# A hybrid decoder layer on one core: each head's values product placed behind the next round's sums of decays

## What is computed

```python
# differential attention, 8 heads, per head h and block of 128 queries
logits = q @ k.T ; logits = where(dist >= 0, logits + bias, -inf)
p = softmax(logits)                         # two maps per head
attn = p[:, :, 0] - lam * p[:, :, 1]
out = attn @ v[:, :kend]                    # the "values product"
...
# state-space branch, 32 heads in 4 groups, chunks of 128 tokens
acs = cumsum(a)                             # a = dt*A: the decays
decay_in = exp(where(causal, acs_l - acs_s, -inf))
y_diag = einsum(cb, decay_in, xs)
```

## Time and profile before

| | us |
|---|---|
| median of 3 runs | 989.04 |
| lowest, highest | 988.66, 990.14 |
| the profiled execution, whole time | 989.82 |
| the profiled execution, span from first to last instruction | 987.7 |
| span of the eight rounds, from the first sums of decays | 154.2 to 288.6 |

### The profile page before, as it was taken

How to read it: one execution, slowest core, us unless ns; L and a number is a source line. 1 busy time by engine, 2 the same in 40 slices (tenths; PEclk the granted TensorE clock), 3 DMA queues, 4 the chain that set the end, 5 groups by cost and what they waited for, 6 DMA issues and landing times.

```text
span 987.7 us, 15502 instructions
## 1 busy us (share of the span) xinstructions
PE 972.6 (98%) x6366; PEld 700.5 (71%) x6367; DVE 516.1 (52%) x1051; ACT 392.1 (40%) x707; POOL 53.4 (5%) x54
## 2 busy tenths in 40 slices
PE   9999999999999999999999999999999999999995
PEld 8999999999999999999984444444444444444342
DVE  6988555767679976765675433223222232222124
ACT  6776435656577743555341122112211221122113
POOL 0000102324200000000000000000000000000000
PEclk9999999999999999999999999999999999999998
DMA  8584534333354554656969999999999999999993
GB/s 315 187 307 174 197 139 140 124 125 126 129 176 166 186 198 172 241 211 255 405 253 362 415 420 419 420 420 420 419 420 420 419 420 420 420 420 420 421 419 122
DMA packets 42982, 292.43 MB, mean 296 GB/s; under 512 B 4760, under 2 KB 6944, under 8 KB 8352
## 3 DMA queue, kind: packets, MB, share of 16 engines
q1 hardware_dynamic: 42128, 286.19, 73.3%
q0 software_dynamic: 784, 5.24, 1.4%
HBM read 290.36 MB, written 2.63 MB: 297 GB/s over the span
## 4 chain that ended last, share of the span: by engine, by line
PE 89%; SPq 5%; DMA 3%; DVE 2%; issue 0%; ACT 0%; DVEq 0%; ACTq 0%
PE stream L1631 33%; PE stream L1988 19%; PE stream L2012 10%; PE stream L1656 9%; PE work L1977 5%; SPq L532 5%; DMA place_w<-in_wstream 3%; PE stream L1998 1%; PE stream L1929 1%; PE work L1755 1%; PE stream L1937 1%; PE stream L1931 1%; PE stream L1935 1%; PE work L1731 1%; PE work L1862 1%; PE work L1844 1%
## 5 line engine op out<-in xcount | busy, mean ns | idle before, releaser
L1032 DVE TENSOR_TENSOR w_lo<-raw,w_hi 128x1024 fp32r<-128x1024 f32 x142 | 172.4, 1233 | 54.0 <-ACT w_hi L699 53.7
L1988 PE MATMUL stream<-ring,xg 128*64 128x512 f32 x640 | 197.3, 593 | 1.7 <-DMA ring<-in_wstream 1.0
L699 ACT ACTIVATE w_hi<-raw 128x1024 fp32r<-128x1024 f32 x142 | 147.3, 1052 | 58.4 <-DMA raw<-in_wdense 41.5
L1631 PE MATMUL stream<-xT_hi,w_hi 128*128 128x256 f32 x560 | 159.4, 285 | 0.0
L1631 PE MATMUL stream<-xT_lo,w_hi 128*128 128x256 f32 x560 | 157.9, 282 | 0.0
L1631 PE MATMUL stream<-xT_hi,w_lo 128*128 128x256 f32 x560 | 157.8, 282 | 0.0
L1988 PEld LDWEIGHTS stream<-ring,xg 128*64 128x64 f32 x640 | 62.6, 137 | 92.2 <-issue 92.2
L1631 PEld LDWEIGHTS stream<-xT_hi,w_hi 128*128 128x128 f32 x560 | 106.1, 190 | 3.7 <-issue 3.1
L1631 PEld LDWEIGHTS stream<-xT_hi,w_lo 128*128 128x128 f32 x560 | 105.9, 189 | 0.0
L1631 PEld LDWEIGHTS stream<-xT_lo,w_hi 128*128 128x128 f32 x560 | 105.6, 189 | 0.0
L1502 DVE TENSOR_TENSOR hh<-h,stream 128x256 f32<-128x256 f32 x32 | 13.5, 421 | 173.3 <-ACT h L961 173.3
(11 more groups left out here) (389 smaller groups left out, 2019.4 us busy)
## 6 DMA issues: line engine op xcount, KB each, us to landing
ring<-in_wstream SPq DMA_DIRECT2D x120, 1024.0 KB, 19.4
raw<-in_wdense SPq DMA_DIRECT2D x72, 1024.0 KB, 4.8
place_e<-in_wstream SPq DMA_DIRECT2D x24, 1024.0 KB, 19.1
place_m<-in_wstream SPq DMA_DIRECT2D x12, 1024.0 KB, 17.6
place_c<-in_wstream SPq DMA_DIRECT2D x12, 1024.0 KB, 19.5
place_w<-in_wstream SPq DMA_DIRECT2D x12, 1024.0 KB, 19.1
place_x<-in_wstream SPq DMA_DIRECT2D x12, 1024.0 KB, 21.2
ln<-in_lnp POOLq DMA_DIRECT2D x3, 1024.0 KB, 7.0
```

The lines of the kernel that those rows point to most:

```text
L699: nc.scalar.activation(w_hi[:, q % ROUNDED, :], raw[:, q % 6, :], ACT.Copy).then_inc(w_rounded, 1)
L1032: tt(w_lo[:, q % 6, :], raw[:, q % 6, :], w_hi[:, q % ROUNDED, :].bitcast(F32), ALU.subtract).then_inc(w_rest, 1)
L1631: last = mm(S[n % 4][:, 0:SEQ], w[:, b, :], a[:, kb, :], start=(kb + j == 0), stop=(kb == chunks * KB - 1 and j == len(parts) - 1))
L1988: last = mm(S[2][e * SLOTS:(e + 1) * SLOTS, :], feature_block(buf, kb)[:, col + e * SLOTS:col + (e + 1) * SLOTS], tiles[e][kb // 4][:, kb ...
```

## The change

The three values products become a function `values(i)`. It is called for head i-1 in round i, behind the sums of decays and in front of the wait for `av_cp`, and once for head 7 behind the loop. Nothing is added or taken away; the wait for `attnT_cp` that the logits had moves into the function.

```diff
+            def values(i):
+                pe.wait_ge(attnT_cp, i + 1)
+                head = slice(i * P, (i + 1) * P)
+                mm(W[1][:, 0:P], attnT[:, 0:P], v[:, 0, head], start=True, stop=True)
+                mm(W[1][:, P:SEQ], attnT[:, P:SEQ], v[:, 0, head], start=True, stop=False)
+                mm(W[1][:, P:SEQ], attnT[:, SEQ:384], v[:, 1, head], start=False, stop=True).then_inc(av_mm, 1)
...
                 if i >= 1:
-                    pe.wait_ge(attnT_cp, i)
+                    values(i - 1)
                     pe.wait_ge(av_cp, i)
...
                 if i == 0:
                     pe.wait_ge(act_took, taken_count(out_index("v", 7)))
-                pe.wait_ge(attnT_cp, i + 1)
-                head = slice(i * P, (i + 1) * P)
-                mm(W[1][:, 0:P], attnT[:, 0:P], v[:, 0, head], start=True, stop=True)
-                mm(W[1][:, P:SEQ], attnT[:, P:SEQ], v[:, 0, head], start=True, stop=False)
-                mm(W[1][:, P:SEQ], attnT[:, SEQ:384], v[:, 1, head], start=False, stop=True).then_inc(av_mm, 1)
+            values(7)
```

## The result

| | before | after |
|---|---|---|
| median of 6 runs each, us | 988.85 | 993.00 |
| lowest, highest, us | 988.54, 990.14 | 991.79, 993.86 |
| ratio after/before, 95% interval | | 1.0039 [1.0026, 1.0052] |
| the profiled execution, whole time, us | 989.82 | 992.59 |
| its span, us | 987.7 | 990.5 |

What follows compares the result with a forecast made beforehand. PE was taken to bound the rounds; seven borders losing 0.55 us each give 3.9 us, carried in full onto the 989.04 us median: 992.9 us, range 991.2 to 994.4 us.

Steps and rivals of the forecast that it cites:

- What bounds the stage: In the eight rounds PE is busy for all 134.51 us, so a microsecond PE stands still is a microsecond lost.
- The wait for `av_cp` cost nothing before: In front of the logits: four sums of decays covered ACT's copy to `o_tok`, leaving 0.45 us of slack.
- the 0.10 us ahead of the logits: Between last sum of decays and logits: 0.10 us beyond the sum's own 0.23, read as a change of operand shape.
- The sum for one border: Between two rounds: logits start 2.37 us behind the last block matmul, not 1.82; 0.55 us lost per border.
- The count of seven borders: Loss occurs for heads 0 to 6, head 7 staying in front of the memory blocks: 7 x 0.55 = 3.9 us.
- ACT's slack: ACT's exponentials of decays begin 0.76 us behind the logits; 0.8 us of slack stay before DVE wants them.
- POOL and DVE: POOL's fourth `a_tri` op and DVE's masks stop colliding; DVE gains 0.8 us in six rounds, valued at nothing.
- The 0.17 us in front of the transposes: Named as a wait for `attn` in seven rounds, taken as shape change; if a real wait, 1.2 us come back.
- The way to the end: Expert transfers are issued behind PE's counters, so the saturated DMA stretch moves with PE; 3.9 us carry over in full.
- first expert product 3.9 us later: Sign of being right, behind the rounds: the first expert product and the last tile landed both come 3.9 us later.
- The third rival: At the logits PE resumes late behind ACT and pays weight loading: 0.15 us more per border, 993.9 us; chance 0.12.
- The page's figure for a single matmul: Result time of the last values record: 219 ns for bf16 against 275 for float32; 0.06 us less per border, 3.5 in all.

Runs made afterwards that it cites:

- four slower kernels: Against the kernel before: values product between the sums, 989.72 us; old order with ACT's copy behind the rounding, 990.92; the change, 993.00; the change with three copies, 998.88.
- row of longer copies: The changed kernel with ACT making the copy to `o_tok` three times, each waiting for the one before: 998.88 us, ratio 1.0100 to the kernel before.
- kernel with the late copy: The kernel before with PE's order untouched; ACT rounds the fourth weight chunk ahead of the copy to `o_tok`: 990.92 us, ratio 1.0022.

## Why the prediction was right, point by point

- **What bounds the stage.** Right: PE had no slack in the rounds, and what was lost in the rounds came out at the end, in the four slower kernels.
- **The wait for `av_cp` cost nothing before.** Right. With the wait moved away, the way from the last block matmul to the logits is 1.81 us, against 1.82 with it in the kernel before; the 0.10 us ahead of the logits are no wait.
- **The sum for one border.** Forecast 2.37 us to the logits, measured 2.35. Its unknown term, how soon PE goes on behind ACT, was taken as 0.08 us between 0.04 and 0.14; it is 0.05 us. Forecast 0.55 us lost per border, measured 0.53; rounds forecast 3.9 us longer, measured 3.65. The count of seven borders is that of the waits. The total, 992.9 forecast and 993.0 measured, is closer than its parts, which is luck: the loss was 4.15 us and not 3.9, and the median of the kernel before came out at 988.85 us and not at 989.04.
- **ACT's slack.** Right: the exponentials of decays start 0.79 us behind the logits (forecast 0.76), and the masks 2.66 us behind them, as before.
- **POOL and DVE.** Right in both: the collision is gone, and by itself it is worth nothing to PE. The 0.17 us in front of the transposes, named as a wait for `attn` in seven rounds before, are a change of shape: after the change the names have swapped, the length has not.

```profile
PEld work L1778 <- issue: 1.2, 7, 0.2
...
PEld work L1778 <- DVE attn L1156: 0.2, 1, 0.2
```

- **The way to the end.** Right in the medians (+4.15 us) and in the row of longer copies (+9.97). In the two profiled executions the end moved by less, 2.8 us in the span, and so did the landing of the last tile, 960.54 before and 963.35 after. The reason is ahead of the change: the first sums of decays start at 154.38 us before and at 153.51 after, 0.87 us earlier, in a stretch that is the same in all kernels and whose length lay between 153.51 and 154.40 in the eight profiled executions. 3.65 - 0.87 = 2.78 us. My item "first expert product 3.9 us later" (it came 3.0 us later) had not allowed for that.
- **The third rival** (PE pays more than the wait) is out for this change: PE resumed in 0.05 us at all seven borders. In the kernel with the late copy it took 0.14 us.
- **Left open.** The medians differ by 0.3 to 0.5 us more than the rounds in each of the four slower kernels. This is within the spread of runs, and was not followed up.

The page's figure for a single matmul (Trainium skill, "TensorE: Matmul & The Clock Gate", "Single matmul latency") is for bf16; the rows' 275 ns for float32 gave the sum that was measured; an estimate by the page's figure would have been 0.4 us less. The rule on the shared port (Trainium skill, "SBUF — State Buffer", "SBUF: two separate sides") agrees with the trace in both directions: 1.56 and 1.52 us where the two ops met, 1.04 and 0.68 where they no longer did.

## To carry to other kernels

Where a bank is written, copied away by another engine and written again, count what stands between the two writers in the queue against the whole loop: result of the last matmul (0.275 us), start of the copy (0.045), copy (0.383), return (0.05), 0.75 us here. Products that are free to be moved are worth most exactly there, and moving them away cost their cover here and nothing else. If an order is wanted for another reason, give the first writer another bank that is idle at that time: that cost nothing and kept the other engines' gain.

## What the runs showed of the hardware

- PE resumed 0.05 us behind the end of ACT's copy in three kernels, with stops of up to 1.30 us, and 0.14 us behind it in the one where the copy followed directly behind a rounding (why is open). ACT started 0.045 us behind a matmul. No other price of these short stops showed, and the granted clock stayed at 1.00 in rounds with seven stops of 0.47 us.
- A change between products of half and of full shape cost PE about 0.15 us: two fewer per round gave 0.29 us per round where nothing waited behind them, and 0.17 us, 1.4 us of the kernel, where the transposes then had to wait for `attn`. It stands in the trace as idle time of the weight loads with no releaser, or with one that had just finished and was not the reason.
- Two ops of POOL and DVE that meet take 1.56 and 1.52 us in place of 1.04 and 0.68. Taking them apart was worth nothing until the products of PE in front of the waiting ones had become shorter; then it was worth 0.12 us in each of six rounds.
